# One decoder layer with 32 experts on one core: when the first expert weights are fetched, in which portions, and where expert 0 gets its up bias

## The reference, cut to what matters

```python
x = x + mixed @ w_out                       # mixer: attention + S5 branch (w_glu 512 x 2048)
h = rmsnorm(x, g_ffn)
gate, chosen = softmax(top4(h @ w_router + b_router))
for e in range(32):                         # tokens gathered for expert e
    gu  = h[rows] @ w_up[e] + b_up[e]       # w_up[e]: 1024 x 2048 float32 = 8.4 MB
    act = (clip(gu[1024:]) + 1) * g * sigmoid(1.702 * g)     # g = min(gu[:1024], 7)
    x[rows] += gate * (act @ w_down[e] + b_down[e])          # w_down[e]: 1024 x 1024 = 4.2 MB
x = x + sigmoid(rmsnorm(x, g_ple_gate) @ w_ple_gate) * rmsnorm(p @ w_ple_proj, g_ple_post)
```

## Time and profile before

| | us |
|---|---|
| median of 3 runs | 1157.62 (1157.17 to 1158.16) |
| the profiled execution | 1157.22 |
| its span in the trace | 1155.5 |
| PE busy | 1112.7 (96%) |
| DVE busy | 391.9 (34%) |
| POOL busy | 169.2 (15%) |
| ACT busy | 161.5 (14%) |

### The profile page before, as it was taken

The page is one execution under the profiler, slowest core; times in us unless marked ns, Lnnn a source line. Parts: engine busy times, 40 slices in busy tenths (PEclk is TensorE's granted clock), DMA queues, the critical chain, the costliest instruction groups (busy, mean ns, idle before and its releaser), DMA issues.

```text
span 1155.5 us, 15655 instructions
## 1 busy us (share of the span) xinstructions
PE 1112.7 (96%) x6453; PEld 489.2 (42%) x6453; DVE 391.9 (34%) x831; ACT 161.5 (14%) x286; POOL 169.2 (15%) x180
## 2 busy tenths in 40 slices
PE   9999999999999999998999999999999999999998
PEld 4578786533433333333333333333333333333344
DVE  6557967522222223221232213212122121212316
ACT  2320112500000000000221111111111111101113
POOL 2998982100000000000000000000000000000005
PEclk9999999999999999999999989999999999999999
DMA  9933248999999999999999999999999999999991
GB/s 316 369 105 142 77 188 333 374 421 429 427 425 437 424 439 431 426 434 433 427 436 432 426 435 432 428 433 434 425 436 433 426 436 432 426 435 427 426 411 41
DMA packets 40864, 441.03 MB, mean 382 GB/s; under 512 B 9797, under 2 KB 10369, under 8 KB 23041
## 3 DMA queue, kind: packets, MB, share of 16 engines
q1 hardware_dynamic: 40240, 439.01, 90.6%
q0 software_dynamic: 480, 1.57, 0.4%
q10 hardware_dynamic: 112, 0.02, 0.0%
HBM read 439.54 MB, written 1.05 MB: 381 GB/s over the span
## 4 chain that ended last, share of the span: by engine, by line
PE 51%; DMA 36%; POOL 8%; DVE 3%; issue 1%; ACT 0%; SPq 0%; DVEq 0%
DMA ring<-in_w_down_dram 24%; PE bank L1874 21%; PE bank L1928 13%; DMA ring<-in_w_up_dram 12%; PE bank L1945 3%; POOL ring L354 3%; PE bank L1691 2%; PE bank L1699 2%; PE bank L1516 2%; PE bank L1739 2%; PE bank L1838 2%; PE bank L2050 2%; POOL ring L614 1%; POOL ring L605 1%; POOL arena L605 1%
## 5 line engine op out<-in xcount | busy, mean ns | idle before, releaser
L1874 PE MATMUL bank<-ring,arena 128*64 128x512 f32 x2040 | 452.2, 600 | 14.6 <-DMA ring<-in_w_up_dram 14.5
L1874 PEld LDWEIGHTS bank<-ring,arena 128*64 128x64 f32 x2040 | 143.7, 138 | 317.7 <-issue 290.0
L1928 PE MATMUL bank<-ring,arena 128*64 128x512 f32 x1024 | 234.9, 612 | 17.6 <-DMA ring<-in_w_down_dram 16.5
L1310 DVE TENSOR_TENSOR arena<-arena,bank 128x512 f32<-128x512 f32 x128 | 79.5, 682 | 292.1 <-PE bank L1945 292.1
L1928 PEld LDWEIGHTS bank<-ring,arena 128*64 128x64 f32 x1024 | 75.2, 140 | 156.7 <-issue 147.3
L1286 DVE TENSOR_SCALAR arena<-bank 128x512 f32<-128x512 f32 x32 | 22.1, 692 | 348.5 <-PE bank L1874 348.5
L664 POOL TENSOR_TENSOR ring<-ring 128x2048 f32<-128x2048 f32 x1 | 4.5, 4546 | 911.4 <-DMA ring<-in_w_ple_gate_dram 911.4
L842 ACT ACTIVATE arena<-arena 128x512 f32<-128x512 f32 x32 | 20.2, 632 | 491.0 <-DVE arena L1286 491.0
L1516 PE MATMUL bank<-arena,ring 128*128 128x256 f32 x384 | 85.9, 382 | 0.4 <-DVE arena L1111 0.4
L1516 PEld LDWEIGHTS bank<-arena,ring 128*128 128x128 f32 x384 | 72.0, 190 | 12.9 <-issue 3.6
L1945 PE MATMUL bank<-arena 64*128 64x512 f32 x256 | 63.5, 614 | 0.0
(11 more groups left out here) (273 smaller groups left out, 795.5 us busy)
## 6 DMA issues: line engine op xcount, KB each, us to landing
ring<-in_w_up_dram SPq DMA_DIRECT2D x40, 4096.0 KB, 33.3
ring<-in_w_down_dram SPq DMA_DIRECT2D x24, 4096.0 KB, 34.8
ring<-in_w_up_dram SPq DMA_DIRECT2D x43, 2048.0 KB, 23.5
ring<-in_w_down_dram SPq DMA_DIRECT2D x15, 2048.0 KB, 15.5
ring<-in_w_in_dram SPq DMA_DIRECT2D x7, 2048.0 KB, 18.2
ring<-in_w_up_dram SPq DMA_DIRECT2D x9, 1024.0 KB, 25.8
ring<-in_w_glu_dram SPq DMA_DIRECT2D x2, 2048.0 KB, 7.6
ring<-in_w_out_dram SPq DMA_DIRECT2D x2, 2048.0 KB, 8.2
```

What stands on the lines that cost most here:

```text
L1310: dve.tensor_tensor(part, part, bank[at][:, :], ALU.add).then_inc(m["sc_add"], 1)
L1874: last = pe.matmul(to, XS[:, k, :], columns, start=False, stop=(k == DT - 1))
L1928: last = pe.matmul(bank[YB][HALF * c:HALF * (c + 1), :], ACTT[:, j, HALF * h:HALF * (h + 1)], piece[:, j, 512 * c:512 * (c + 1)], start=(h ...
```

## The change

1. **The first nine pieces** are issued in the order 2, 0, 1, 3, 4, 5, 6, 8, 7, without the wait for y3. Piece 2 waits for g7; pieces 0 and 1 for POOL's last product with the table in their place (`back_set` 31 and 32); piece 3 for a3. Half of (2,0) is issued directly behind piece 3. Pieces 6, 8 and 7 are loaded in halves, each half as of the output product that frees it.
2. **`w_glu`** is split by columns: each of its two places holds both halves (value and gate) of four of the eight glu jobs, in 2 loads of 1 MiB each. Piece 4 then waits for glu3, piece 5 for glu7.
3. **Refills in halves:** besides (1,3), the pieces (1,4), (2,1) and (2,3) are loaded in halves, the first as soon as the first half of what was there has been read (`head_read` 2, 3 and 4).
4. **Fewer small loads:** `GPOST` is loaded as one row of 4 KB and spread in `embeddings` by two products with a row of ones and two ACT copies; `BDOWN` in two loads in place of four; `WPP` and `PIN` are laid out so that `WPP` has 8 KB rows.
5. **`up_bias` of expert 0** is laid down behind its up products (they start the accumulation, the bias closes it), in front of the `gather` of expert 1; the other experts are as before.

```diff
-                     ("glu", 0): "glu7", ("glu", 1): "glu7", ...
+                     ("glu", 0): "glu3", ("glu", 1): "glu7", ...
+        AHEAD = {(1, 0): 0, (1, 1): 0, (1, 2): 0}
+        BEHIND = {(1, 3): 1, (1, 4): 2, (2, 1): 3, (2, 3): 4}
+        PARTED = {**AHEAD, **BEHIND}
...
+                elif key[0] == "glu":
+                    for h, sem in enumerate((arrived[at], S["glu_gate_in"])):
+                        cols = slice(D * h + 512 * key[1], D * h + 512 * (key[1] + 1))
+                        sp.dma_start(place(at).rearrange("p (k h n) -> p k h n", k=WT, h=2)[:, :, h, :],
+                                     w_glu[0, :, cols].rearrange("(k p) n -> p k n", p=P)).then_inc(sem, 16)
...
-            released(sp, "y3")
-            for i in (0, 1, 2, 3, 4, 5, 6, 8, 7):
+            for i in (2, 0, 1, 3, 4, 5, 6, 8, 7):
                 at = spot(0, i)
-                if at == TURN["out", 0][0]:
-                    wait_full(sp, "outb")
-                    sp.wait_ge(S["w_sum"], 4)
-                elif at == TURN["out", 1][0]:
-                    wait_full(sp, "outa")
+                piece = expert_source(i // PER_EXPERT, i % PER_EXPERT)
+                if divmod(i, PER_EXPERT) in AHEAD:
+                    for h in range(2):
+                        at_once = h
+                        if at == TURN["out", 0][0]:
+                            if h == 0:
+                                sp.wait_ge(S["prod_full"], 1)
+                                sp.wait_ge(S["w_sum"], 4)
+                            else:
+                                wait_full(sp, "outb")
+                        elif at == PLACES - 1:
+                            sp.wait_ge(S["prod_full"], 2 + h)
+                        elif h == 0:
+                            wait_full(sp, "outc")
+                            at_once = 1
+                        else:
+                            wait_full(sp, "outa")
+                            at_once = 0
+                        cols = slice(at_once * PLACE // 2, (at_once + 1) * PLACE // 2)
+                        sp.dma_start(place(at)[:, cols], piece[:, cols]).then_inc(arrived[at], 16)
+                    continue
+                if at < 2:
+                    sp.wait_ge(S["back_set"], 2 * TILES - 1 + at)
...
                 if i == 3:
                     sp.dma_start(place(at)[:, 0:2048], piece[:, 0:2048]).then_inc(arrived[at], 16)
+                    sp.dma_start(place(spot(2, 0))[:, 2048:], expert_source(2, 0)[:, 2048:]).then_inc(S["ahead_in"], 16)
                 else:
                     load_rows(at, piece)
-            sp.dma_start(place(spot(2, 0))[:, 2048:], expert_source(2, 0)[:, 2048:]).then_inc(S["ahead_in"], 16)
...
-            sp.dma_start(GPOST, g_ple_post[0:1, :].broadcast_to([P, D])).then_inc(S["ple_in"], 16)
+            sp.dma_start(GPOST[0:1, :], g_ple_post[0:1, :]).then_inc(S["ple_in"], 16)
...
-            sp.dma_start(WPP, w_ple_proj[0].rearrange("(k p) n -> p k n", p=P)).then_inc(S["ple_in"], 16)
+            sp.dma_start(WPP, w_ple_proj[0].rearrange("(p k) n -> p k n", p=P)).then_inc(S["ple_in"], 16)
...
-                if isinstance(n, int) and (n, c) == (1, 3):
-                    sp.wait_ge(S["head_read"], 1)
-                else:
+                if isinstance(n, int) and (n, c) in BEHIND:
+                    sp.wait_ge(S["head_read"], BEHIND[n, c])
+                    sp.dma_start(place(spot(n, c))[:, 0:PLACE // 2], expert_source(n, c)[:, 0:PLACE // 2]).then_inc(
+                        arrived[spot(n, c)], 16)
                     left(n, c)
+                    sp.dma_start(place(spot(n, c))[:, PLACE // 2:], expert_source(n, c)[:, PLACE // 2:]).then_inc(
+                        arrived[spot(n, c)], 16)
+                    return
...
+                for c, at in enumerate((YB, WTB)):            # ACT, in embeddings
+                    act.wait_ge(S["pp_full"], 2 * TB + c + 1)
+                    act.activation(GPOST[:, 512 * c:512 * (c + 1)], bank[at][:, :], ACT.Copy).then_inc(S["pp_set"], 1)
...
-            vacant(UG, UU)                                    # PE, ahead of rk1
-            pe.wait_ge(S["up_bias_set"], 4)
-            up_bias(M, 0)
...
+                if first:                                     # PE, at the end of up(M, 0)
+                    pe.wait_ge(S["up_bias_set"], 4)
+                    up_bias(m, n, closing=True)
...
+                        if isinstance(n, int) and (n, h, j) == (0, 0, 1):    # PE, in down
+                            last.then_inc(S["head_read"], 1)
...
+                pe.wait_ge(S["pp_set"], 2 * TB)               # PE, at the end of embeddings
+                for c, at in enumerate((YB, WTB)):
+                    pe.matmul(bank[at][:, :], ONES[0:1, :], GPOST[0:1, 512 * c:512 * (c + 1)], start=True,
+                              stop=True).then_inc(S["pp_full"], 1)
```

More of the change, by code:

```diff
@@ L262, in hybrid_layer @@
         LAST_READ = {("in", 3): "u1", ("in", 0): "q1", ("in", 1): "k1", ("in", 2): "v1", ("attn", 0): "a3",
-                     ("glu", 0): "glu7", ("glu", 1): "glu7", ("out", 0): "out4", ("out", 1): "out4"}
+                     ("glu", 0): "glu3", ("glu", 1): "glu7", ("out", 0): "out4", ("out", 1): "out4"}
         LAST_READ.update({("in", 4 + i): f"g{2 * i + 1}" for i in range(4)})
@@ L285, in loads @@
                     if not (n < E and c % 2 and together(n, c - 1)):
-                        count[spot(n, c)] += 1
+                        count[spot(n, c)] += 1 + ((n, c) in PARTED)
                         last[n, c] = count[spot(n, c)]
@@ L435, in _ @@
                     wait_full(sp, held[at])
-                src = source(key)
+                src = None if key[0] == "glu" else source(key)
                 if key == ("in", 0):
@@ L491, in _ @@
             sp.dma_start(AWAY_U, expert_source(0, 3)[:, 3072:].rearrange("p (r n) -> p r n", r=2)).then_inc(S["away_in"], 16)
-            sp.dma_start(GPOST, g_ple_post[0:1, :].broadcast_to([P, D])).then_inc(S["ple_in"], 16)
+            sp.dma_start(GPOST[0:1, :], g_ple_post[0:1, :]).then_inc(S["ple_in"], 16)
             sp.dma_start(PIN, p[0, 0].rearrange("(t p) n -> p t n", p=P)).then_inc(S["ple_in"], 16)
-            for g in range(4):
-                rows = slice(E * g, E * (g + 1))
-                sp.dma_start(BDOWN[rows, :], b_down[0, :, 512 * (g % 2):512 * (g % 2 + 1)]).then_inc(S["down_bias_in"], 16)
+            for c in range(2):
+                sp.dma_start(BDOWN[E * c:E * (c + 1), :], b_down[0, :, 512 * c:512 * (c + 1)]).then_inc(S["down_bias_in"], 16)
             wait_full(sp, "lg1")
-            sp.dma_start(WPP, w_ple_proj[0].rearrange("(k p) n -> p k n", p=P)).then_inc(S["ple_in"], 16)
+            sp.dma_start(WPP, w_ple_proj[0].rearrange("(p k) n -> p k n", p=P)).then_inc(S["ple_in"], 16)
             def left(n, c):
@@ L1680, in _ @@
             s5_out(3)
-            arrive(("glu", 0))
-            arrive(("glu", 1))
             for i in range(DT):
+                if i % 4 == 0:
+                    arrive(("glu", i // 4))
+                    pe.wait_ge(S["glu_gate_in"], 32)
+                held = weight(("glu", i // 4), WT).rearrange("p k (h n) -> p k h n", h=2)
                 b = take(f"glu{i}")
                 for h in range(2):
-                    m = i + DT * h
                     for k in range(WT):
@@ L1690, in _ @@
                             pe.wait_ge(S["gelu_set"], k + 1)
-                        last = pe.matmul(b[:, SEQ * h:SEQ * (h + 1)], weight(("glu", k // 2), 2)[:, k % 2, P * m:P * (m + 1)],
+                        last = pe.matmul(b[:, SEQ * h:SEQ * (h + 1)], held[:, k, h, P * (i % 4):P * (i % 4 + 1)],
                                          GY[:, k, :], start=(k == 0), stop=(k == WT - 1))
@@ L1738, in up_bias @@
                         rows = slice(E * (2 * w + h), E * (2 * w + h + 1))
-                        pe.matmul(bank[UG + w][HALF * h:HALF * (h + 1), :], PICK[rows, :], BUP[rows, :], start=True, stop=False)
+                        last = pe.matmul(bank[UG + w][HALF * h:HALF * (h + 1), :], PICK[rows, :], BUP[rows, :],
+                                         start=not closing, stop=closing)
+                    if closing:
+                        last.then_inc(m[("up_g", "up_u")[w]], 1)
             def gather_first(t, ds):
@@ L1873, in up @@
                                     columns = AWAY_U.rearrange("p r (m h j) -> p h r m j", h=2, j=4)[:, h]
-                                last = pe.matmul(to, XS[:, k, :], columns, start=False, stop=(k == DT - 1))
-                            if k == DT - 1:
+                                last = pe.matmul(to, XS[:, k, :], columns, start=(first and k == 0),
+                                                 stop=(k == DT - 1 and not first))
+                            if k == DT - 1 and not first:
                                 last.then_inc(m[("up_g", "up_u")[w]], 1)
-                        if first and k == 0:
```

(4 more changed lines are left out.)

24 lines of the change are left out of this document (9 added, 15 removed).

## The result

| | before | changed |
|---|---|---|
| median of 7 runs, us | 1157.62 (1156.99 to 1158.16) | 1161.52 (1160.22 to 1162.24) |
| the profiled execution, us | 1157.22 | 1161.68 |
| its span, us | 1155.5 | 1159.9 |
| MB moved | 441.03 | 440.38 |

A forecast was written before the change was run, and what follows sets the result against it. The DMA stream was taken to bound the kernel from 224 on. Gain 2.4 us less 1.5 lost again, less 0.1 for halves: net 0.8, so 1156.8 us for a median; range 1154.6 to 1159.0.

The forecast's parts named there:

- The gain on offer: At the first refills, (1,3) on: they begin to flow at 223.9 instead of 226.3, a gain of 2.4 us.
- The walk: Refill queue followed piece by piece from 223.9: empty 1.1 us at (2,1) and 0.4 at (2,2), 1.5 us lost again.
- bias shift: Down of expert 0 starts later with the bias behind up; bounds 0 to 1.3 us, 0 giving 1.8 in all.
- 0.9 MB undone: Bytes still ahead of (1,3) at 224 in the kernel before, by byte count: 2.2 us at 421 GB/s.
- The halves: Refills in halves: without them the changed kernel would lose 1.5 us more through holes at (2,1) to (2,4).
- The sign that the DMA would be idle from 165 to 172: Expected in the changed kernel's trace: DMA share near 0 from about 165 to 172.
- The cross-check by two landings: Landings of half of (2,0) and of WPP, each less 1.5 us, taken to confirm refills flowing from 226.3.
- the remainder of 0.02: Chance of 0.02 kept for a gain from a source the prediction didn't see.
- the clock's term of 3 us: Half clock after PE's standstill ahead of rk1: places free up to 3.0 us later; left out of the forecast sum.
- the series: Bias laid behind expert 0's up products: UU complete 1.0 us later, down starting 1.0 to 1.3 us later.
- Rival (c): Slower by PE's clock, half clock as expert 0 starts: 1159.8 us, or 1158.5 at 1.7 us; chance 0.09.
- Embeddings, w_glu, the extra halves: Some 3 us more in embeddings, covered by queued transfers; w_glu in 2 KB rows nothing; six new halves 0.1 us.

The follow-up runs named there:

- e1: The changed kernel with part 5 alone undone, the up bias of expert 0 ahead of rk1 again: 1155.84 us, ratio 0.9985.
- e10: e1 with all of part 1 undone (old order, waits and portions of the first nine pieces), the new w_glu split kept: 1155.68 us, ratio 0.9984.
- e5: e1 with the refills (1,4), (2,1) and (2,3) whole again, (1,3) still in halves: 1156.89 us, ratio 0.9995.
- e7: The kernel before with part 3 alone done, refills (1,4), (2,1) and (2,3) in halves: 1157.24 us, ratio 0.9996.
- e6: e1 with the first six pieces issued late again, in the order and behind the waits of the kernel before: 1155.71 us, ratio 0.9984.
- e11: The kernel before with expert 0's up bias behind its up products and the gap ahead of rk1 filled with the same 8 instructions: 1159.06 us, ratio 1.0017.
- e9: The changed kernel with the up bias of expert 0 left out altogether: 1158.18 us, ratio 1.0007.
- e2: The kernel before with part 5 alone done, expert 0's up bias behind its up products: 1161.2 us, ratio 1.0028.
- e3: The changed kernel with the gap ahead of rk1 filled by the 8 bias products once more, overwritten by up: 1158.25 us, ratio 1.0007.
- e4: The changed kernel with half the filling ahead of rk1, 4 bias instructions (w = 0 only): 1159.4 us, ratio 1.0018.
- e8: e1 with the small loads as before (gain broadcast to 128 partitions, four bias loads), WPP keeping 8 KB rows: 1156.13 us, ratio 0.9987.

## Why the prediction was wrong, point by point

**What bounds the kernel: right.** The DMA stream does, from the first refill on, and its beginning hangs on PE reading expert 0. Bytes worth 4.5 us are missing by 300 in the changed kernel, and its span is 4.4 us longer.

**The gain on offer: right. The walk behind it: right in its sum, by luck in part.** With a bias shift of zero the prediction gave 1.8 us (its own terms, 2.4 less 0.4 less 0.1, make 1.9); e1 measured 1.7, e10 1.6. `WPP` went out at 216.73 and the queue was empty from about 222.2, as forecast. By bytes of the pieces e1 was 2.5 us ahead of the kernel before at 228 (forecast: 2.4; both rest on the 0.9 MB undone, which is good to 0.5), but 1.1 less at 240 and 1.6 less at 300. Of these 1.6 the walk had 0.5; the rest goes with the slow flow of a shallow queue, which it didn't have (see the last section). The profiled execution of e1 is 0.7 us below that of the kernel before, the medians are 1.7 apart, and why they differ so is open. The halves were worth 1.5 us in the walk and 1.35 in e5, and nothing alone in e7. That the filled breaks before 222 are no prize of their own: e6, e10. The sign that the DMA would be idle from 165 to 172 was wrong (402 to 407 GB/s there in e1 and the changed kernel) and changed nothing; from 181 to 187 it was idle, as forecast.

Three readings of the prediction are weaker than it made them. That the kernel before never runs empty was true, but its margin at (2,1) was 0.5 us, not 2.2 (e11). The cross-check by two landings can't tell 226.3 from a later begin: it takes 226.3 to get the 1.5 us and then takes the 1.5 us off to get 226.3. And the 2 us of fixed time in the Trainium skill (DMA: Bandwidth & Descriptors, section "Anatomy of one DMA") are given there for transfers issued from GpSimd; here SP issues them, and no run measures what of 1.5 us lies behind the last byte. The chances, taken with the remainder of 0.02, add up to 1.02.

**The forecast fell on part 5, in two terms.** The first is the clock. The prediction saw the standstill (1.1 + 0.3 us ahead of rk1; measured 1.29), saw what half clock would do (up to 3.0 us; measured 3.3 by expert 0's second k, and 3.0 at down in e9), and gave it 0.09, since "it decides from a standstill of over 2 us". That threshold was the faulty step, and the clock's term of 3 us stood at nothing in the forecast because of it. It was read from three waits inside long streams: 1.71 and 1.59 us kept full clock there, 2.60 did not the earlier trace rows. The trace of the kernel before had more of them, which say that no such threshold can be read from waits:

```profile
816.11 8.66 PE L1874 MATMUL bank<-ring,arena 128*64 128x512 f32 x32 [2.32 <-DMA ring<-in_w_up_dram]
...
874.46 7.09 PE L1874 MATMUL bank<-ring,arena 128*64 128x512 f32 x32 [2.31 <-DMA ring<-in_w_up_dram]
```

The same wait ahead of the same work lowered the clock once and once not. The 1.71 us that the prediction counts as safe lowered it in eight of the other traces, and 2.81 us ahead of the down at 947.7 left it full in the changed kernel, 2.60 ahead of the one at 504.5 in e1. Besides, the stretch ahead of rk1 is made otherwise: transposes, logits and gathers of 0.2 to 0.7 us with waits of 0.17 and 0.27 us between them already. There 1.29 us were enough, in e2 and e9 as well (1.29 and 1.30). The Trainium skill (TensorE: Matmul & The Clock Gate, section "A second HAM failure mode: psum-queue depth-cycling") tells of a kernel of large bf16 products in which short, frequent idle times between groups of products make the clock swing. The trace agrees in that short idle times suffice, with 1.29 us and 0.50 from 219 on, though the clock fell here once and didn't swing. I should have weighed it as a rival of more than a tenth.

The second is the series. The step read "down starts 1.0 to 1.3 us later"; it was 2.0 to 2.1 (e3, e11), with a full clock. I had added the bias to the time of U and let DVE's chain follow unchanged. But the closing bias also delays G, by 1.9 us where U is delayed by 1.0 (G was done first; both without the 0.36 us that up came later in e3), and so takes away the overlap by which DVE had clipped it: PE waits 0.83 us.

**The prices in time.** Rival (c) was put at 1159.8 with its bias shift of 1.1 us in it, and the range ended below that, at 1159.0. Clock (2.65 us over e1 in e9) and series (2.4 us in e3) add up to 5.0; the changed kernel is 5.6 above e1. On a queue that has just been emptied a delay of PE passes through to the end nearly whole, and 4.9 us late at down cost 4.4 of span. The prediction's own walk, fed with the times at which the changed kernel asked for its pieces (225.08, 244.73 and 249.88), gives a loss of 3.1 us: the flow begins 0.4 later than before, and the holes at (2,1) and (2,2) are 2.4 and 0.2. Measured are 3.9. The 0.8 us between them are of the size of what the shallow queue takes, but no run settles them.

**Embeddings, w_glu, the extra halves: right.** Their costs are not to be found; from 300 to 1100 both kernels move the same 428 to 432 GB/s in every 100 us.

## What to carry to other kernels

Work on PE that looks free to move may be what keeps its clock up: before taking products out of a stretch of short ones with waits, ask what the engine does there instead, and keep the gap filled or fill it with products that are thrown away (e3 took back 3.2 us so). Don't read a safe length of wait from one trace: here the same wait of 1.71 us kept the clock in six traces and lowered it in eight. Moving work behind a long product adds more than its duration, if it closes two results together that used to come one after the other: the eight bias products, on different parts of the array, ended together. And where a ring is full, earlier loads are worth only what they clear away before the first place comes free; the margin that hides a late reader is the margin at the tightest refill, not the work undone at the start.

## What the runs showed of the hardware that I had not expected

**The clock.** It fell to 0.50 behind a standstill of 1.29 us in a stretch of short products, 0.3 to 1.0 us after the products began again (at 218.2 in e2, 218.4 in e9, 219.0 in the changed kernel), and came back 6.8 us later each time. It also fell with a standstill of 0.29 us, when the gap was filled with four products on half of the array's parts (e4), where eight held it in the trace of e3, though the records show PE equally busy (1.07 and 1.09 us). And behind the same wait of 1.71 us it fell in eight traces of 14. So between two executions of the same work it can go either way. What decides is open.

**A shallow queue flows more slowly without looking idle.** In 228 to 240 e1 (halves) moved 394 GB/s and e5 (whole pieces) 392, at DMA shares of 1.00 and 0.97; with transfers queued behind one another it was 430 at 1.03 (e7) and 433 in the kernel before. e10 (401) and e8 (422), whose queues were fuller at 222, lie between. That it is the depth of the queue is my reading of these six; no run sets the depth by itself. The line of e1:

```profile
228.00:240.00 12.00, 1.00 1.00 394
```

A busy share of 1 is thus no proof that the DMA moves all it could. By bytes this eats about 1 us of what the walk gives e1 in that stretch.
